# High-part products of a weight chunk first, low part waited for in mid chunk, in a split-precision decoder layer

## The chip, the core and the metric

The kernel runs on one core of one Trainium2 chip. The metric is the device time of one execution in microseconds, median of several runs. "Before" is the kernel without the change.

## What is computed

One inference step of one decoder layer, all in float32: 512 prompt tokens and 8 samples of one new token each, model width 1024.

```python
mod = silu(c) @ w_ada + b_ada                       # 9 vectors per sequence: shift, scale, gate x 3
x = x + 0.5 * ga1 * swiglu(rms_mod(x, g1, sh1, sc1), wf1i, wf1o)
h, state = mixer(rms_mod(x, g2, sh2, sc2), ...)     # RG-LRU branch and mLSTM branch, merged, projected
x = x + ga2 * h
x = x + 0.5 * ga3 * swiglu(rms_mod(x, g3, sh3, sc3), wf2i, wf2o)
y = rms(x, g_final)
```

`swiglu` is an up-projection to 2 x 2816 columns, silu of one half times the other, and a down-projection back to 1024. `w_ada` is 1024 x 9216.

## The kernel before, in words

**Layout.** Activations stand with features on the 128 partitions and all 520 tokens along the free side, in 8 row blocks of 128 features. Weights come from memory in chunks of 128 output columns: a chunk holds up to 8 blocks of 128 x 128, 512 KB.

**Split precision.** Every weight and activation is split into a high part in the fast matmul format and a low part, the rest. A product is high x high + high x low + low x high. SP loads a chunk into `raw` (line 418), ACT copies it into `w_h` (`split`, line 946, the copy on 955; in one place in two halves, 954 and 955), DVE subtracts it into `w_l` (`split`, line 1347, on 1354 and 1357). All three have a ring of 3 slots. ACT signals `w_hi_ready`, DVE `w_lo_ready`; both count chunks in order. SP loads the next chunk into a slot after DVE's signal, ACT overwrites `w_h` after TensorE's signal `chunk_done` of the chunk that used the slot before.

**Products.** `product` (line 585) multiplies one chunk with all 520 tokens, in two halves of 260 that lie in two PSUM banks of an accumulator tile `big`. For each row block it makes six matmuls: (w_h, x_h), (w_h, x_l), (w_l, x_h), each for two halves, 48 for 8 blocks. It waits for `w_lo_ready` ahead of everything (line 587), then for the accumulator to be emptied, and, where a list `ready` is given, ahead of each row block for the low part of the activations (line 594). Two accumulators alternate.

**Condition products.** `modulation` (line 610) makes one column block of `mod`: the silu of the conditions, 18 columns, is the stationary operand, a block of 128 weights moves, 16 matmuls a chunk, high and low part in turn (line 616), after a wait for `w_lo_ready` (line 613).

**Order of the work.** All engines run the same chunk list by hand-written loops. At the start, 17 of the 72 condition blocks are made from unsplit weights (line 691) while the first norm is computed; the first two chunks of the first up-projection have a function of their own (`first_products`, line 727). The first up-projection then runs 11 turns of 9 chunks in the order P M P M P M P M M (P a product, M a condition product; the first turn P P M M P M P M M). In a turn ACT splits chunk k+2 at step k; at step 7 it splits the next turn's first P in two halves. The first down-projection follows: 8 output tiles in three chunks of 8, 8 and 6 row blocks; the third chunk of every second tile has a `ready` list with one and the same value for its six blocks. Then the mixer, 81 chunks in straight-line code with the small matmuls of recurrence and attention between them (`small_job`; the recurrence gates are line 845), the second up-projection (44 P; the first P of each turn of 6 has a `ready` list), the second down-projection. The first two chunks after each norm of the residual are in `unnormalised` (line 632), with `ready`-like waits of its own. POOL, with the stored states and the first rows after a norm, waits in two places for `chunk_done`.

Of the kernel before, what the change touches and what calls it, by code (L numbers as in the profile page):

```python
# [20 lines left out]
P = 128  # L21
D = 1024
KT = D // P
# [3 lines left out]
HALF = T // 2  # L27
# [13 lines left out]
RING = 3  # L41
# [150 lines left out]
def build(nc, xT, cT, w_ada, b_ada, ff1_in, ff1_out, w_mix, ff2_in, ff2_out, vecs, conv_w, w_rg,  # L192
# [3 lines left out]
    with ctx:  # L196
        def sb(name, shape, dt=F32, stack=ctx):
            return stack.enter_context(nc.sbuf_tensor(name, shape, dt))

        def sem(name):  # L200
            return ctx.enter_context(nc.semaphore(name))
# [6 lines left out]
        w_h = [sb(f"w_h{i}", [P, KT * P], F32R) for i in range(RING)]  # L208
        w_l = [sb(f"w_l{i}", [P, KT * P], F32R) for i in range(RING)]
# [110 lines left out]
        w_hi_ready = sem("w_hi_ready")  # L320
        w_lo_ready = sem("w_lo_ready")
        chunk_done = sem("chunk_done")
# [261 lines left out]
        def _(pe):  # L584
            def product(c, c_expr, t, t_half, xh, xl, k0, n, first=True, last=True, ready=None):

                pe.wait_ge(w_lo_ready, c_expr + 1)
                if first and not (isinstance(t_half, int) and t_half == 0):
                    pe.wait_ge(evac[t % 2], t_half)
                out = big[t % 2]  # L590
                wh, wl = w_h[c % RING], w_l[c % RING]
                for i in range(n):
                    if ready is not None:
                        pe.wait_ge(lo_ready, ready(k0 + i))
                    w = slice(i * P, (i + 1) * P)
                    for s, (a, b) in enumerate(((wh, xh), (wh, xl), (wl, xh))):
                        for hf in range(2):
                            ins = nc.tensor.matmul(out[:, hf, 0:HALF], a[:, w],  # L598
                                                   b[:, k0 + i, hf * HALF:(hf + 1) * HALF],
                                                   start=first and i == 0 and s == 0,  # L600
                                                   stop=last and i == n - 1 and s == 2)
                ins.then_inc(chunk_done, 1)
# [7 lines left out]
            def modulation(c, c_expr, out, n):  # L610


                pe.wait_ge(w_lo_ready, c_expr + 1)
                for kt in range(KT):
                    for s, w in enumerate((w_h[c % RING], w_l[c % RING])):
                        ins = nc.tensor.matmul(out[0:NR, n * P:(n + 1) * P], cs_hl[:, kt, :],  # L616
                                               w[:, kt * P:(kt + 1) * P],
                                               start=kt == 0 and s == 0, stop=kt == KT - 1 and s == 1)
                ins.then_inc(chunk_done, 1)
# [123 lines left out]
            def ffn(cb, tbase, pattern, loops, s_xn, s_hid):  # L743
# [15 lines left out]
                def turn(i, pattern=pattern, k0=0):  # L759
                    n = a = 0  # L760
                    for k, kind in enumerate(pattern):
                        c = cb + k
                        if k < k0:
                            n += 1
                            continue
                        back = k == TURN_BACK and "M" in pattern and not (isinstance(i, int) and i == 0)
                        if back:
                            backs(i, "wait")
                        if kind == "P":
                            t = tbase + n  # L770
                            product(c, i * len(pattern) + c, t, i * (n_p // 2) + t // 2, xn_h, xn_l, 0, KT,
                                    ready=xn_split if k == 0 and not first else None)
                            n += 1
                        else:
                            g = sum(a >= t0 + size for t0, size in MOD_GROUPS)
                            m = M_ADA1 + g
                            if a == MOD_GROUPS[g][0]:
                                pe.wait_ge(taken[m % BANKS], i + m // BANKS)
                            modulation(c, i * len(pattern) + c, bank[m % BANKS], a - MOD_GROUPS[g][0])
                            a += 1  # L780
                        if back:
                            backs(i, "work")
# [16 lines left out]
                with pe.Fori(0, KT // 2) as i:  # L799
                    for jj in range(2):  # L800
                        for k, (k0, n) in enumerate(FFO_CHUNKS):
                            product(cb + 3 * jj + k, i * 6 + (cb + 3 * jj + k), tbase + jj,
                                    i + (tbase + jj) // 2, hid_h, hid_l, k0, n, first=k == 0, last=k == 2,
                                    ready=(lambda kt: s_hid + FT) if k == 2 and jj == 0 else None)
# [108 lines left out]
            for i, (what, j) in enumerate(MIX):  # L913
                if what == "bra":
                    xh, xl, base = hb_h, hb_l, S_HA
                elif what == "brb":
                    xh, xl, base = hb_h, hb_l, S_HB
                elif what == "out":
                    xh, xl, base = mg_h, mg_l, S_MG
                else:  # L920
                    xh, xl, base = xn_h, xn_l, S_XN2 + 1
                t = T_MIX + i
                if i == PRE:
                    product(C_MIX + i, C_MIX + i, t, t // 2, xh, xl, 0, KT, ready=lambda kt: S_XN2 + USABLE[kt])
                elif i > PRE:
                    product(C_MIX + i, C_MIX + i, t, t // 2, xh, xl, 0, KT, ready=(lambda kt: base + kt + 1)
                            if i == FIRST_OF[what] and what in ("bra", "brb", "out") else None)
                for key in AFTER[i]:
                    small_job(key)
# [1098 lines left out]
```

## Time and profile before

| | |
|---|---|
| median of 3 runs | 1464.92 us (1464.09 to 1465.06) |
| the profiled execution, its own time | 1464.09 us |
| its span, first to last instruction | 1462.3 us |
| TensorE matmul records | 1419.7 us, 11964 matmuls |
| DVE, ACT, POOL busy | 729.5, 558.8, 68.8 us |
| mean granted TensorE clock | 0.994 |

A matmul record reaches from its start to a modelled end, and records of successive matmuls overlap, so TensorE's busy time is not a measure of how well it is used; the distance between starts is. Idle time "before" an instruction is the gap to the end of the engine's last record, with the engine whose signal ended it.

### The profile page before, as it was taken

Reading aid. Unit: us, or ns where it says so; the run is one execution under the profiler, and the core shown is the slowest. Engines: PE = TensorE matmul, PEld = TensorE weight load, DVE = VectorE, ACT = ScalarE, POOL = GpSimd, SP = SyncE. Lnnn points to the kernel's source line nnn. Section 1 sums busy time; section 2 is a strip of 40 time slices with the busy share of each in tenths; the row PEclk is TensorE's granted clock in tenths of the full one; section 3 lists DMA queues with packets and bytes.
Section 4 is the critical chain, followed back from the end, with each engine's and each line's share of the span. In section 5 each row is a group of like instructions: output and inputs, shape, how many; then the busy total and the mean of one; then the engine's idle time right before and its main releaser. Section 6 shows DMA issues by size and latency. Waiting matters only on the chain.

```text
span 1462.3 us, 29304 instructions
## 1 busy us (share of the span) xinstructions
PE 1419.7 (97%) x11964; PEld 1384.7 (95%) x11964; DVE 729.5 (50%) x1250; ACT 558.8 (38%) x813; POOL 68.8 (5%) x135
## 2 busy tenths in 40 slices
PE   5999999999999989999999999999999999999996
PEld 4899999999999989999998989999999999999996
DVE  4645454455344665774475666744673333333333
ACT  4433444443232557723443435432452322221211
POOL 1000000000000300000011201200010000000000
PEclk9999999999999999999999999999999999999998
DMA  9455555555323422233253525432223223223321
GB/s 373 135 165 161 161 167 165 159 158 166 89 88 93 141 69 73 73 92 115 68 157 116 166 80 166 140 100 87 87 87 98 89 86 97 90 82 94 88 80 59
DMA packets 49588, 174.01 MB, mean 119 GB/s; under 512 B 6608, under 2 KB 6672, under 8 KB 49136
## 3 DMA queue, kind: packets, MB, share of 16 engines
q1 hardware_dynamic: 43200, 151.68, 33.5%
q0 software_dynamic: 6032, 19.25, 4.0%
q10 hardware_dynamic: 288, 2.13, 0.4%
q8 instruction: 49, 0.80, 0.2%
q14 instruction: 19, 0.16, 0.0%
HBM read 161.28 MB, written 11.75 MB: 118 GB/s over the span
## 4 chain that ended last, share of the span: by engine, by line
PE 90%; DVE 5%; ACT 2%; issue 1%; DMA 1%; POOL 0%; SPq 0%; DVEq 0%; ACTq 0%; POOLq 0%
PE big L598 79%; PE bank L616 2%; PE bank L885 2%; PE bank L877 1%; PE bank L891 1%; PE big L645 1%; DVE w_l L1357 1%; DMA adaw<-w_ada 1%; PE bank L845 1%; PE bank L909 1%; PE bank L864 0%; ACT w_h L954 0%; DVE tb L1918 0%; PE bank L691 0%; DVE tb L1561 0%
## 5 line engine op out<-in xcount | busy, mean ns | idle before, releaser
L1357 DVE TENSOR_TENSOR w_l<-raw,w_h 128x1024 fp32r<-128x1024 f32 (+2 forms) x272 | 321.5, 1186 | 355.4 <-ACT w_h L955 351.0
L598 PE MATMUL big<-xn_h,w_h 128*128 128x260 f32 x2224 | 452.9, 285 | 5.5 <-DVE w_l L1357 2.7
L598 PE MATMUL big<-xn_l,w_h 128*128 128x260 f32 x2224 | 449.7, 283 | 0.0
L598 PE MATMUL big<-xn_h,w_l 128*128 128x260 f32 x2224 | 448.1, 282 | 0.0
L955 ACT ACTIVATE w_h<-raw 128x1024 fp32r<-128x1024 f32 (+2 forms) x272 | 276.3, 1020 | 237.7 <-PE big L598 236.4
L598 PEld LDWEIGHTS big<-xn_h,w_h 128*128 128x128 f32 x2224 | 344.2, 188 | 9.6 <-issue 4.2
L598 PEld LDWEIGHTS big<-xn_h,w_l 128*128 128x128 f32 x2224 | 343.5, 188 | 0.0
L598 PEld LDWEIGHTS big<-xn_l,w_h 128*128 128x128 f32 x2224 | 343.3, 188 | 0.0
L598 PE MATMUL big<-hid_h,w_h 128*128 128x260 f32 x704 | 142.2, 283 | 0.0
L598 PE MATMUL big<-hid_h,w_l 128*128 128x260 f32 x704 | 141.5, 282 | 0.0
L598 PE MATMUL big<-hid_l,w_h 128*128 128x260 f32 x704 | 141.5, 282 | 0.0
L598 PEld LDWEIGHTS big<-hid_l,w_h 128*128 128x128 f32 x704 | 108.7, 188 | 0.0
L598 PEld LDWEIGHTS big<-hid_h,w_l 128*128 128x128 f32 x704 | 108.4, 188 | 0.0
L598 PEld LDWEIGHTS big<-hid_h,w_h 128*128 128x128 f32 x704 | 108.3, 188 | 0.0
L1476 DVE TENSOR_TENSOR tb<-tb,big 128x520 f32<-128x520 f32 x43 | 29.9, 696 | 124.3 <-PE big L598 124.3
L1052 ACT ACTIVATE tb<-big 128x520 f32<-128x520 f32 x43 | 26.0, 605 | 169.7 <-PE big L598 169.3
L616 PE MATMUL bank<-w_h,cs_hl 128*18 128x128 f32 x440 | 57.4, 223 | 0.5 <-DVE w_l L1357 0.5
L616 PE MATMUL bank<-w_l,cs_hl 128*18 128x128 f32 x440 | 57.3, 223 | 0.0
L968 ACT ACTIVATE tb<-x 128x520 f32<-128x520 f32 (+1 forms) x24 | 15.3, 639 | 104.7 <-DVE x L1458 82.0
L598 PE MATMUL big<-hb_h,w_h 128*128 128x260 f32 x256 | 51.7, 283 | 0.4 <-DVE ma L1877 0.4
L598 PE MATMUL big<-hb_h,w_l 128*128 128x260 f32 x256 | 51.5, 283 | 0.0
L598 PE MATMUL big<-hb_l,w_h 128*128 128x260 f32 x256 | 51.4, 282 | 0.0
(338 smaller groups left out, 1449.7 us busy)
## 6 DMA issues: line engine op xcount, KB each, us to landing
raw<-ff_in SPq DMA_DIRECT2D x88, 512.0 KB, 3.6
raw<-w_mix SPq DMA_DIRECT2D x81, 512.0 KB, 3.6
raw<-w_ada SPq DMA_DIRECT2D x55, 512.0 KB, 3.7
raw<-ff_out SPq DMA_DIRECT2D x32, 512.0 KB, 3.5
adaw<-w_ada SPq DMA_DIRECT2D x17, 512.0 KB, 14.2
cst_c<-st_C POOLq DMA_DIRECT2D x32, 256.0 KB, 4.4
o_Cs<-cst_c POOLq DMA_DIRECT2D x32, 256.0 KB, 3.4
raw<-ff_out SPq DMA_DIRECT2D x16, 384.0 KB, 3.2
```

The costliest lines, as they stand in the source:

```text
L598: ins = nc.tensor.matmul(out[:, hf, 0:HALF], a[:, w], b[:, k0 + i, hf * HALF:(hf + 1) * HALF], start=first and i == 0 and s == 0, stop=las ...
L616: ins = nc.tensor.matmul(out[0:NR, n * P:(n + 1) * P], cs_hl[:, kt, :], w[:, kt * P:(kt + 1) * P], start=kt == 0 and s == 0, stop=kt == KT ...
L645: ins = nc.tensor.matmul(big[t % 2][:, hf, 0:ZH], a[:, w], b[:, kt, hf * ZH:(hf + 1) * ZH], start=kt == 0 and s == 0, stop=kt == KT - 1 an ...
L845: ins = nc.tensor.matmul(out[:, 0:HALF], wrg[:, 0 if kind == "rga" else 1, a, :], rg_u[a % RG_BUFS][:, b * HALF:(b + 1) * HALF], start=Tru ...
L877: ins = nc.tensor.matmul(out[:, b * P:NP_], k_t[h % 2][:, dt, b * P:(b + 1) * P], q_t[h % 2][:, dt, b * P:NP_], start=dt == 0, stop=dt == ...
L885: ins = nc.tensor.matmul(out[:, c * P:NP_], lhs, dmat[:, c, c * P:NP_], start=c == 0, stop=c == CH - 1)
L891: ins = nc.tensor.matmul(out[:, 0:HD + 1], ktok[:, c, b * P:(b + 1) * P], vtok[:, c, :], start=c == 0, stop=c == CH - 1)
L955: A(w_h[c % RING][:, from_:width], raw[:, c % RING, from_:width], ACT.Copy).then_inc(w_hi_ready, 1)
L968: A(tb[2][:, :], x[:, kt, :], ACT.Square).then_inc(sq_ready, 1)
L1052: A(two(tb[0][:, :]), slot_view(t), ACT.Silu).then_inc(evac[t % 2], 1)
L1357: V.tensor_tensor(w_l[c % RING][:, from_:width], raw[:, c % RING, from_:width], w_h[c % RING][:, from_:width], ALU.subtract).then_inc(w_lo ...
L1476: V.tensor_tensor(two(tb[1][:, :]), two(tb[0][:, :]), slot_view(t), ALU.mult).then_inc(evac[t % 2], 1)
```

## The change

In `product`, where no `ready` list is given, the wait at the top is for the high part, all matmuls with `w_h` run first, then the wait for the low part, then all matmuls with `w_l`. With a `ready` list nothing changes. In `modulation` all eight matmuls with `w_h` run after a wait for the high part and the eight with `w_l` after a wait for the low part. `first_products` and `unnormalised` stay as they were. Number, shapes and operands of the matmuls stay the same.

```diff
             def product(c, c_expr, t, t_half, xh, xl, k0, n, first=True, last=True, ready=None):
 
-                pe.wait_ge(w_lo_ready, c_expr + 1)
+                pe.wait_ge(w_lo_ready if ready is not None else w_hi_ready, c_expr + 1)
                 if first and not (isinstance(t_half, int) and t_half == 0):
                     pe.wait_ge(evac[t % 2], t_half)
                 out = big[t % 2]
                 wh, wl = w_h[c % RING], w_l[c % RING]
+                if ready is None:
+                    for i in range(n):
+                        w = slice(i * P, (i + 1) * P)
+                        for b in (xh, xl):
+                            for hf in range(2):
+                                nc.tensor.matmul(out[:, hf, 0:HALF], wh[:, w],
+                                                 b[:, k0 + i, hf * HALF:(hf + 1) * HALF],
+                                                 start=first and i == 0 and b is xh, stop=False)
+                    pe.wait_ge(w_lo_ready, c_expr + 1)
+                    for i in range(n):
+                        w = slice(i * P, (i + 1) * P)
+                        for hf in range(2):
+                            ins = nc.tensor.matmul(out[:, hf, 0:HALF], wl[:, w],
+                                                   xh[:, k0 + i, hf * HALF:(hf + 1) * HALF],
+                                                   start=False, stop=last and i == n - 1)
+                    ins.then_inc(chunk_done, 1)
+                    return
                 for i in range(n):
                     if ready is not None:
                         pe.wait_ge(lo_ready, ready(k0 + i))
...
             def modulation(c, c_expr, out, n):
 
 
-                pe.wait_ge(w_lo_ready, c_expr + 1)
-                for kt in range(KT):
-                    for s, w in enumerate((w_h[c % RING], w_l[c % RING])):
+                for s, (ready, w) in enumerate(((w_hi_ready, w_h[c % RING]), (w_lo_ready, w_l[c % RING]))):
+                    pe.wait_ge(ready, c_expr + 1)
+                    for kt in range(KT):
                         ins = nc.tensor.matmul(out[0:NR, n * P:(n + 1) * P], cs_hl[:, kt, :],
                                                w[:, kt * P:(kt + 1) * P],
                                                start=kt == 0 and s == 0, stop=kt == KT - 1 and s == 1)
```

## Rows read from the trace of the kernel before

**Rows 1.** The page: busy time by engine, and the chain that ended last.
```profile
PE 1419.7 (97%) x11964; PEld 1384.7 (95%) x11964; DVE 729.5 (50%) x1250; ACT 558.8 (38%) x813; POOL 68.8 (5%) x135
...
PE 90%; DVE 5%; ACT 2%; issue 1%; DMA 1%; POOL 0%; SPq 0%; DVEq 0%; ACTq 0%; POOLq 0%
```
**Rows 2.** TensorE's waits: line, released by: us in total, times, longest us.
```profile
PE bank L845 <- ACT rg_r L1191: 5.8, 2, 4.4
PE big L598 <- DVE w_l L1357: 2.7, 11, 0.6
```
**Rows 3.** Timeline at a turn's border: start us, length us, engine, line; idle before in brackets.
```profile
95.39 0.61 ACT L955 ACTIVATE w_h<-raw 128x512 fp32r<-128x512 f32 x1
...
96.13 0.68 DVE L1357 TENSOR_TENSOR w_l<-raw,w_h 128x512 fp32r<-128x512 f32 x1
...
96.51 0.22 PE L616 MATMUL bank<-w_l,cs_hl 128*18 128x128 f32 x1
...
96.94 0.50 PE L598 MATMUL big<-xn_h,w_h 128*128 128x260 f32 x2 [0.21 <-DVE w_l L1357]
...
97.28 0.40 PE L598 MATMUL big<-xn_l,w_h 128*128 128x260 f32 x2
```
**Rows 4.** Timeline of TensorE in the turn before, at a border without a wait.
```profile
88.77 0.22 PE L616 MATMUL bank<-w_l,cs_hl 128*18 128x128 f32 x1
88.82 0.46 PE L598 MATMUL big<-xn_h,w_h 128*128 128x260 f32 x2
89.12 0.40 PE L598 MATMUL big<-xn_l,w_h 128*128 128x260 f32 x2
...
94.41 0.41 PE L598 MATMUL big<-xn_h,w_l 128*128 128x260 f32 x2
```
**Rows 5.** The chain that ended last, in order of time: first products of turns.
```profile
67.92 6.03 PE big L598 x48
...
96.94 6.04 PE big L598 x48
...
329.26 6.05 PE big L598 x48
```
**Rows 6.** Timeline at the start of the first up-projection.
```profile
48.80 2.05 ACT L955 ACTIVATE w_h<-raw 128x1024 fp32r<-128x1024 f32 x2
...
49.88 1.23 DVE L1357 TENSOR_TENSOR w_l<-raw,w_h 128x1024 fp32r<-128x1024 f32 x1 [0.97 <-ACT w_h L955]
...
50.43 0.23 PE L616 MATMUL bank<-w_l,cs_hl 128*18 128x128 f32 x1
...
51.16 0.24 PE L616 MATMUL bank<-w_h,cs_hl 128*18 128x128 f32 x1 [0.51 <-DVE w_l L1357]
...
52.91 0.39 PE L598 MATMUL big<-xn_h,w_h 128*128 128x260 f32 x1 [0.60 <-DVE w_l L1357]
```
**Rows 7.** Timeline, first down-projection: first pairs of third chunks and of the chunks after them.
```profile
371.37 0.40 PE L598 MATMUL big<-hid_h,w_h 128*128 128x260 f32 x2
...
375.70 0.40 PE L598 MATMUL big<-hid_h,w_h 128*128 128x260 f32 x2
...
387.23 0.40 PE L598 MATMUL big<-hid_h,w_h 128*128 128x260 f32 x2
...
391.56 0.40 PE L598 MATMUL big<-hid_h,w_h 128*128 128x260 f32 x2
```
**Rows 8.** Chain piece in the mixer; busy time of L598 in the second up-projection (PE, PEld, clock, DMA).
```profile
605.81 34.59 PE big L598 x288
...
1078.37:1318.87 240.50, 240.50 (x1993) 240.50 (x1993) 1.00 0.31 93
```
**Rows 9.** Recurrence gates by the timeline; a stretch by engine (PE, PEld, DVE, ACT, POOL, clock, DMA).
```profile
542.71 1.92 PE L845 MATMUL bank<-ma,wrg 128*128 128x260 f32 x8
...
549.02 3.49 PE L845 MATMUL bank<-ma,wrg 128*128 128x260 f32 x8 [4.40 <-ACT rg_r L1191]
...
549.40:552.80 3.40, 3.40 (x11) 2.79 (x10) 0.70 (x1) 2.25 (x6) 0.00 (x0) 0.50 0.43 143
```

## The prediction, made before the change was run

> **What bounds the kernel now.** The page first: TensorE is busy for 97% of the span and the chain that ended last runs over it for 90% [rows 1]. So the time is the sum of the matmuls plus the moments in which TensorE stands still, and a change that leaves every matmul in place can only win those moments back. I therefore read TensorE's list of waits next. Its largest waits on ACT lie at L845, in the recurrence gates of the mixer, which the change does not touch. On the low part of a weight chunk (w_l, made by DVE at L1357) the products at L598 wait 11 times, for 2.7 us in all [rows 2]; the condition products at L616 wait once more, 0.51 us [rows 6].
>
> That sum is too small, and the timeline says why. Matmul records overlap: pairs follow each other every 0.24 us while each pair's record lasts 0.40 us [rows 4]. An idle time is counted from the end of the record before, so about 0.16 us of each stop is invisible. I go by starts. At a border without a wait, the last condition matmul starts at 88.77, the product's first pair at 88.82 and its second at 89.12: 0.05 and 0.30 us [rows 4]. At a border with a wait the same steps take 96.51 to 96.94 and on to 97.28: 0.43 and 0.34 us [rows 3]. The stop costs 0.38 + 0.04 = 0.42 us, twice the 0.21 that the row shows as idle.
>
> Where these borders are: each turn of the first up-projection ends in two condition chunks in a row, which give ACT and DVE only 2 us for splitting the next product's weights. There are ten such borders (after each turn but the last), the first at 67.92, then nine from 96.94 to 329.26 at a distance of 29.04 us [rows 5]. The other two waits are at the start: the second condition chunk (51.16 after 50.43) and the product after it (52.91) [rows 6]. That makes the 11 and the one; no later product waits for w_l.
>
> **The change, part by part.**
>
> *First wait moved from low to high part.* At a border TensorE would be free at 96.51 + 0.06 = 96.57. The second half of the high part is written by ACT from 95.39 to 96.00 [rows 3], so 0.57 us before it is wanted; the low part is ready at 96.81. ACT and DVE are tied to the end of an earlier product, not to the start of this one, so this cover does not shrink when TensorE gets ahead. Each border then looks like 88.82, and I take 10 x 0.42 = 4.2 us.
>
> *Second wait, in mid chunk.* The low part is now asked for after 32 matmuls of 0.12 us, at 96.57 + 3.84 = 100.4, some 3.6 us after it is there. Behind that wait stand 16 matmuls and the chunk's completion signal, for which ACT and DVE (eviction, splitting into the slot that comes free) and one POOL wait are queued; with 3.6 us in hand none of them is delayed. If the cover went, the old wait would come back whole, 0.42 us a border. DMA issues are released by DVE's splits alone and move in no queue.
>
> *Condition chunks.* Eight matmuls with the high part (8 x 0.06 = 0.48 us) now come before the wait. It binds only at the second chunk: high part ready at about 49.83 (half of ACT's pair from 48.80), TensorE free at 50.49, high half to 50.97, then the low part, which DVE ends at 51.11. As before it starts at 51.16, but only eight matmuls are left: done at 51.64. The next product's high part was finished at 50.85, so it starts at 51.64 and not at 52.91: 1.27 us, and 0.04 for its first step as above, 1.31 together [rows 6].
>
> *A satisfied wait.* Every product without a readiness list and every condition chunk gets one more wait: 42 + 20 + 75 + 35 + 20 = 192 products and 55 condition chunks. What does one cost when it is satisfied? The down-projection answers: its third chunk of 36 matmuls has a wait before each of the six row blocks in one of two output tiles and none in the other. With six waits it takes 371.37 to 375.70, without 387.23 to 391.56, 4.33 us each [rows 7]. I take nothing. A rule of the Trainium skill can be held against this: TensorE: Matmul & The Clock Gate, Part 2, step 1, says that TensorE draws weight loads ahead of matmuls in flight, and a wait in mid stream is where that could stop. By the rows the sum stays at nothing; by the rule, read that way, every new wait would expose a load (priced as a rival below). [Rows 7] speak for the former.
>
> *The order itself.* Loads and matmuls are the same in kind and number: each matmul loads its weights anew before and after. What could shift is the step between matmuls. It is not constant: 34.59 us for 288 in the mixer, 0.1201, but 240.50 for 1993 in the second up-projection, 0.1207 [rows 8]; 89.12 to 94.41 for 44 is 0.1202 [rows 4]. Same shapes, same order, two values; nothing in the trace says which the new order gets. I take no change, being between the ends. If all went to 0.1207, the reordered 7440 matmuls outside the second up-projection would cost 7440 x 0.0006 = 4.4 us; if all went to 0.1200, 1680 x 0.0007 + 2016 x 0.0002 = 1.6 us would be won.
>
> *The clock.* After TensorE's 4.40 us stop at 549 us the granted clock is 0.50 (1.2 GHz) for 3.4 us, and eight matmuls take 3.49 us that took 1.92 just before [rows 9]. All of this arrives 5 us earlier afterwards, and the fall may be missed or be met at another stop: about 2 us either way (1.57 on these eight, the rest on the product behind them). I count nothing.
>
> **Sum:** 4.2 + 1.31 = 5.5 us less. The profiled execution took 1464.09 (span 1462.3 and 1.8 around it), hence 1458.6. The median of the three runs is 0.83 above it, so I forecast **1459.4**. Its own range is 1459.4 - 1.6 - 2 to 1459.4 + 2.
>
> **The rivals.**
>
> 1. *The step turns slow.* The new order falls into the slower of the two steps everywhere: 1459.4 + 4.4 = 1463.8, within 0.2% of before. For it: the first products after a stop in the second up-projection start a slow stretch that never ends. Against: most stretches run at the fast one. Chance 0.10.
>
> 2. *The wait moves to the high part.* If ACT were more than 0.57 us later at the borders, the product would wait for w_h as long as for w_l now; only the 1.31 us of the start would stay: 1463.6. Against: its order of work does not change. Chance 0.03.
>
> 3. *The other side: each mid-chunk wait exposes a weight load, even when satisfied.* Place: the seam between high and low part of all 192 products. Price: after a stop the first step is 97.28 - 96.94 = 0.34 for a pair and not 0.24 [rows 3, 4], so 0.10 us a seam, 19.2 us; condition chunks at 0.04 add 2.2. That would give 1459.4 + 21.4 = 1480.8. It decides from (5.5 + 2.9) / 247 = 0.034 us a wait. Against it stand the six waits that cost nothing [rows 7]; for it, that those were on a signal long given, while this one is given 3.6 us before. Chance 0.05.
>
> 4. *It does not do what it says*: the borders wait for something else behind w_l, such as the eviction of the accumulator. By the code that tile is emptied before the product ahead of the border ends, so chance 0.02; 1464.9.
>
> **How the numbers follow.** 0.80 is left for the forecast. 0.2% of 1464.9 is 2.9 us, about what a measurement can tell from no change: under 1462.0 counts as faster. The forecast's own range, 1455.8 to 1461.4, lies under that, rivals 1, 2 and 4 within 0.2% of before, rival 3 above: faster 0.80, same 0.15, slower 0.05. The range runs from the low end, 1455.8, to 1463.9, which takes in rivals 1 and 2 and leaves out 3 and 4.
>
> **What the profile after would show.** Right: no wait of L598 or L616 on w_l but for one short one at 51 us; product starts 28.6 us apart from turn to turn and not 29.04; the first product at 51.6; chunks elsewhere as long as before. Wrong: a step over 0.24 us between the last pair with the high part and the first with the low part in every chunk (rival 3); the same chunk lengths at 0.1207 a matmul in the mixer (rival 1); a wait on w_h at the turn borders (rival 2). The forecast falls if the turns keep 29.0 us, or if the time after 360 us grows.

## The result, and the profile after

| | before | after |
|---|---|---|
| time, median (lowest to highest), us | 1464.99 (1464.09 to 1467.37, 4 runs) | 1454.4 (1453.1 to 1456.43, 4 runs) |
| profiled execution / its span, us | 1464.09 / 1462.3 | 1453.86 / 1452.1 |

The ratio is 0.9926, with a 95% interval of 0.9909 to 0.9944. The change is faster by 10.6 us: the direction is as forecast, the gain about twice the forecast 5.5, and the time 1.4 us under the low end of the range.

In the changed kernel the reordered products are L597 (high part) and L604 (low part), products with a readiness list L615, condition products L633, the split L972 (ACT) and L1374 (DVE), the recurrence gates L862. First the page, busy times and the chain that ended last:

```profile
PE 1412.8 (97%) x11964; PEld 1379.8 (95%) x11964; DVE 729.4 (50%) x1250; ACT 559.2 (39%) x813; POOL 68.6 (5%) x135
...
PE 92%; DVE 4%; ACT 2%; issue 1%; DMA 1%; POOL 0%; SPq 0%; ACTq 0%; DVEq 0%; POOLq 0%
```

Beside [rows 1], the number of matmuls and loads is the same, yet TensorE's busy time fell by 6.9 us. Waits account for little of that. Of the forecast's 5.5 us, 2.7 + 0.5 stood as idle time before [rows 2, 6], and only the other 2.3, hidden under the overlap of records, can leave the busy time. This row alone says that something else than the waits moved. The waits of TensorE after (line, released by, us in total, times, longest):

```profile
PE bank L862 <- ACT rg_r L1208: 5.8, 2, 4.4
...
PE big L754 <- DVE w_l L1374: 0.4, 1, 0.4
PE big L597 <- DVE ma L1894: 0.4, 1, 0.4
```

The 11 waits of [rows 2] on w_l are gone; the only one on w_l left in the list is that of the very first products (L754), whose code the change doesn't touch. A border of the first up-projection on the timeline, the one that [rows 3] show before:

```profile
92.31 0.61 ACT L972 ACTIVATE w_h<-raw 128x512 fp32r<-128x512 f32 x1
...
93.05 0.68 DVE L1374 TENSOR_TENSOR w_l<-raw,w_h 128x512 fp32r<-128x512 f32 x1
...
93.48 0.45 PE L597 MATMUL big<-xn_h,w_h 128*128 128x260 f32 x2
93.77 0.40 PE L597 MATMUL big<-xn_l,w_h 128*128 128x260 f32 x2
...
97.36 2.09 PE L604 MATMUL big<-xn_h,w_l 128*128 128x260 f32 x16
```

The product starts at 93.48, 0.25 us before DVE has ended the low part (93.05 + 0.68 = 93.73), with no idle time in brackets; the low part is wanted at 97.36, 3.6 us after it is there. Its first step is 0.29 us as at the borders of [rows 4]. From 93.48 eight more turns lead to 321.51, so they are 228.03 / 8 = 28.50 us apart, where 28.6 was forecast and 29.04 stood before [rows 5]. Now the start, which [rows 6] show before:

```profile
29.66 0.51 PE L754 MATMUL big<-xn_h,w_h 128*128 128x260 f32 x2 [0.44 <-DVE w_l L1374]
...
49.34 0.64 PE L633 MATMUL bank<-w_h,cs_hl 128*18 128x128 f32 x8
50.02 0.65 PE L633 MATMUL bank<-w_l,cs_hl 128*18 128x128 f32 x8
50.51 0.45 PE L597 MATMUL big<-xn_h,w_h 128*128 128x260 f32 x2
```

The product that began at 52.91 begins at 50.51, 2.40 us earlier. The short wait that was forecast at 51 us is there, hidden under the overlap of records: the last line of L633 starts 0.68 us behind the one ahead of it, where eight matmuls take 0.48. Not all of the 2.40 us is the change's: the very first products already begin at 29.66 and not at 30.80, ahead of anything that was changed. The chain of before, then that of after (start, length), and the windows around the four matmuls of L704 (before) and L721 (after); in a window the third number from the end is the granted clock:

```profile
2.83 11.93 DMA adaw<-w_ada
...
27.52 1.06 PE bank L704 x4
```
```profile
2.92 11.27 DMA adaw<-w_ada
...
26.85 0.60 PE bank L721 x4
```
```profile
27.20:28.50 1.30, 1.30 (x13) 0.72 (x5) 0.00 (x0) 0.98 (x2) 0.00 (x0) 0.50 1.01 403
```
```profile
26.85:27.45 0.60, 0.60 (x8) 0.43 (x12) 0.00 (x0) 0.60 (x1) 0.00 (x0) 1.00 1.01 403
```

Half of the 1.14 us is a transfer that ended at 14.19 and not at 14.76. The other half is the clock: before, it fell to 0.50 here, and four small matmuls took 1.06 us that took 0.60 after, at 1.00; the rest of the half lies on those just ahead of them. The change gave 2.40 - 1.14 = 1.26 us here, where 1.27 was forecast (1.31 with the product's first step).

So the waits gave what was expected of them: ten borders 4.24 us by their starts (one 0.435, nine 0.371, and 0.047 on each first step), with the start 5.5. The other half is in the steps between matmuls. A window from the first matmul of one chunk to the first of a later one, divided by the matmuls between, gives the mean step. The rows (window; length; busy time and count of PE, PEld, DVE, ACT, POOL; granted clock, DMA share, GB/s) are 20 chunks of the mixer (960 steps), 41 chunks of the second up-projection (1968) and seven output tiles of the second down-projection (924). Before:

```profile
938.65:1053.92 115.27, 115.27 (x963) 115.27 (x961) 63.49 (x107) 37.84 (x55) 3.19 (x6) 1.00 0.33 100
1081.34:1318.87 237.53, 237.53 (x1971) 237.53 (x1969) 79.04 (x85) 67.36 (x91) 0.00 (x0) 1.00 0.31 94
1324.64:1435.71 111.07, 111.07 (x926) 111.07 (x925) 36.44 (x56) 25.95 (x30) 0.00 (x0) 1.00 0.28 82
```

After, the same chunks:

```profile
930.19:1045.18 114.99, 114.99 (x962) 114.99 (x961) 63.53 (x107) 37.84 (x55) 3.18 (x6) 1.00 0.34 101
1072.59:1308.23 235.64, 235.64 (x1970) 235.64 (x1969) 79.06 (x85) 67.31 (x91) 0.00 (x0) 1.00 0.31 95
1313.97:1424.56 110.59, 110.59 (x926) 110.59 (x925) 36.43 (x56) 25.95 (x30) 0.00 (x0) 1.00 0.28 82
```

There is no wait in any of these windows, before or after: TensorE is busy for the whole of each, at full granted clock, with the same work on the other engines. Still the second up-projection goes from 237.53 / 1968 = 120.70 to 119.74 ns a step, the down-projection from 120.21 to 119.69, the mixer from 120.07 to 119.78. Over the whole kernel, chunk by chunk, that is 5.4 us: second up-projection 1.9, mixer 1.2, first up-projection 1.2, the two down-projections 0.55 each.

The balance of the two profiled executions: 1.1 (landing and clock at the start) + 1.3 (waits at the start) + 4.2 (borders) + 5.4 (steps) = 12.0 us less, and 1.9 more, of the clock at two later places (below): 10.1, against 10.2 between the spans.

### The profile page after: what moved, and what is told of

Read it like the earlier page. It is cut to its first block, busy times and chain, and to the rows that moved or that the text cites. A ratio compares the mean times of both kernels' runs of the same rounds, so it can differ in the third digit from the quotient of the medians.

```text
span 1452.1 us, 29304 instructions
## 1 busy us (share of the span) xinstructions
PE 1412.8 (97%) x11964; PEld 1379.8 (95%) x11964; DVE 729.4 (50%) x1250; ACT 559.2 (39%) x813; POOL 68.6 (5%) x135
## 4 chain that ended last, share of the span: by engine, by line
PE 92%; DVE 4%; ACT 2%; issue 1%; DMA 1%; POOL 0%; SPq 0%; ACTq 0%; DVEq 0%; POOLq 0%
PE big L597 49%; PE big L604 24%; PE big L615 6%; PE bank L633 4%; PE bank L902 2%; PE bank L894 1%; PE bank L908 1%; PE big L662 1%; DMA adaw<-w_ada 1%; PE bank L862 1%; PE bank L926 1%; PE bank L881 0%; DVE tb L1935 0%; PE bank L708 0%; PE big L754 0%
## 5 line engine op out<-in xcount | busy, mean ns | idle before, releaser
L1374 DVE TENSOR_TENSOR w_l<-raw,w_h 128x1024 fp32r<-128x1024 f32 (+2 forms) x272 | 321.6, 1187 | 347.9 <-ACT w_h L972 343.6
L597 PE MATMUL big<-xn_h,w_h 128*128 128x260 f32 x2096 | 424.4, 284 | 0.0
L597 PE MATMUL big<-xn_l,w_h 128*128 128x260 f32 x2096 | 422.6, 283 | 0.0
L972 ACT ACTIVATE w_h<-raw 128x1024 fp32r<-128x1024 f32 (+2 forms) x272 | 276.3, 1020 | 236.7 <-PE big L604 231.5
L597 PEld LDWEIGHTS big<-xn_h,w_h 128*128 128x128 f32 x2096 | 324.0, 189 | 1.5
L597 PEld LDWEIGHTS big<-xn_l,w_h 128*128 128x128 f32 x2096 | 323.0, 189 | 0.0
L604 PE MATMUL big<-xn_h,w_l 128*128 128x260 f32 x2096 | 273.2, 283 | 0.0
L604 PEld LDWEIGHTS big<-xn_h,w_l 128*128 128x128 f32 x2096 | 261.2, 188 | 0.0
L597 PE MATMUL big<-hid_h,w_h 128*128 128x260 f32 x608 | 122.1, 282 | 0.0
L597 PE MATMUL big<-hid_l,w_h 128*128 128x260 f32 x608 | 121.9, 282 | 0.0
L597 PEld LDWEIGHTS big<-hid_h,w_h 128*128 128x128 f32 x608 | 93.4, 188 | 0.0
L597 PEld LDWEIGHTS big<-hid_l,w_h 128*128 128x128 f32 x608 | 93.4, 188 | 0.0
L604 PE MATMUL big<-hid_h,w_l 128*128 128x260 f32 x608 | 79.2, 282 | 0.0
L604 PEld LDWEIGHTS big<-hid_h,w_l 128*128 128x128 f32 x608 | 75.7, 188 | 0.0
L597 PE MATMUL big<-hb_h,w_h 128*128 128x260 f32 x224 | 45.2, 283 | 0.4 <-DVE ma L1894 0.4
L597 PE MATMUL big<-hb_l,w_h 128*128 128x260 f32 x224 | 45.1, 282 | 0.0
L1077 ACT ACTIVATE hid_h<-tb 128x520 f32 (+1 forms) x43 | 27.3, 635 | 37.1 <-DVE tb L1493 37.1
L633 PE MATMUL bank<-w_l,cs_hl 128*18 128x128 f32 x440 | 35.3, 222 | 0.0
```

What stands on the lines that cost most here:

```text
L597: nc.tensor.matmul(out[:, hf, 0:HALF], wh[:, w], b[:, k0 + i, hf * HALF:(hf + 1) * HALF], start=first and i == 0 and b is xh, stop=False)
L604: ins = nc.tensor.matmul(out[:, hf, 0:HALF], wl[:, w], xh[:, k0 + i, hf * HALF:(hf + 1) * HALF], start=False, stop=last and i == n - 1)
L972: A(w_h[c % RING][:, from_:width], raw[:, c % RING, from_:width], ACT.Copy).then_inc(w_hi_ready, 1)
L1077: A(hid_h[:, i * (n_p // 2) + (t - tbase) // 2, :], tb[1][:, :], ACT.Copy).then_inc(hi_ready, 1)
L1374: V.tensor_tensor(w_l[c % RING][:, from_:width], raw[:, c % RING, from_:width], w_h[c % RING][:, from_:width], ALU.subtract).then_inc(w_lo ...
```

## The experiments

Theory 1 was: the waits gave what was forecast, and the other half is the order of the matmuls, which shortens the step by itself; theory 2 is its rival. Theories 3 to 7 came up as the runs went on; each expectation says what its theory gives. Steps are mean distances between the starts of matmuls within chunks, in ns.

**Order alone.** The change with all waits back where they were (the edit is against the changed kernel, as are all below that don't say otherwise; where a loop is rewritten, only the new lines that matter are shown):

```diff
-                pe.wait_ge(w_lo_ready if ready is not None else w_hi_ready, c_expr + 1)
+                pe.wait_ge(w_lo_ready, c_expr + 1)
...
-                    pe.wait_ge(w_lo_ready, c_expr + 1)
...
-                for s, (ready, w) in enumerate(((w_hi_ready, w_h[c % RING]), (w_lo_ready, w_l[c % RING]))):
-                    pe.wait_ge(ready, c_expr + 1)
+                pe.wait_ge(w_lo_ready, c_expr + 1)
+                for s, w in enumerate((w_h[c % RING], w_l[c % RING])):
```

> The order of the change with the waits of before: product and condition chunk wait for the low part at the top, then all high-part matmuls, then all low-part ones. Theory 1 (two gains that add: the waits some 5.5 us, and a shorter step between matmuls that comes from the order alone): about 1460 us, 0.997 of before; the twelve waits on w_l are back, the step is 119.6 ns in the second up-projection and 119.5 in the second down-projection. Theory 2 (the step is shorter because of the late wait, which lets the engine run ahead): as before, 1465 us, step 120.7 and 120.2 ns.

1459.58 us (1459.02 to 1461.2, 6 runs), ratio 0.9969 (0.9957 to 0.9981): 4.9 us less than the 1464.49 of before beside it. Its waits on w_l, and its window over the second up-projection:

```profile
PE big L597 <- DVE w_l L1373: 2.9, 11, 0.6
```
```profile
1079.22:1314.86 235.64, 235.64 (x1971) 235.64 (x1969) 79.03 (x85) 67.33 (x91) 0.00 (x0) 1.00 0.31 95
```

The eleven waits stand as in [rows 2], and the window is that of the change to the hundredth.

**Waits alone.** Matmuls in the old order, waits as in the change (the low part is asked for ahead of the first matmul that uses it):

```diff
+                    steps = [(l, b, i, hf) for i in range(n) for l, b in ((0, xh), (0, xl), (1, xh)) for hf in range(2)]
...
+                        if is_l and not waited:
+                            pe.wait_ge(w_lo_ready, c_expr + 1)
...
-                for s, (ready, w) in enumerate(((w_hi_ready, w_h[c % RING]), (w_lo_ready, w_l[c % RING]))):
-                    pe.wait_ge(ready, c_expr + 1)
-                    for kt in range(KT):
+                pe.wait_ge(w_hi_ready, c_expr + 1)
+                for kt in range(KT):
+                    for s, (ready, w) in enumerate(((w_hi_ready, w_h[c % RING]), (w_lo_ready, w_l[c % RING]))):
+                        if kt == 0 and s == 1:
+                            pe.wait_ge(w_lo_ready, c_expr + 1)
```

> The order of before, row block by row block, with the waits of the change: high part at the top, low part ahead of the first matmul that uses it (after 4 matmuls of a product, after 1 of a condition chunk). At a turn's border the low part is ready at 96.81 and would be asked for at 96.57 + 0.48, so the border waits go; the condition chunk at 51 us keeps its wait. Theory 1: 4.2 at the borders and 1.31 - 0.48 at the start, 5.0 us less than before, about 1460 us, step as before (120.7 ns in the second up-projection, 120.2 in the down-projection). Theory 2: 1454.5 us, step 119.6 and 119.5 ns.

1459.52 us (1458.57 to 1460.01, 6 runs), ratio 0.9965 (0.9953 to 0.9977): 5.0 us less. In its second up-projection:

```profile
1077.08:1314.60 237.52, 237.52 (x1970) 237.52 (x1969) 79.04 (x85) 67.36 (x91) 0.00 (x0) 1.00 0.31 94
```

The window is that of before. So 4.9 + 5.0 = 9.9 us make up the 10.6 of the change within their intervals, and neither half needs the other: theory 1 holds, theory 2 falls. Four matmuls of cover (0.48 us) give at the borders all that 32 give: in both kernels the product starts there 0.06 us behind the last condition matmul. At the start they give less: counted from the very first products, the next product begins 0.45 us later than with the change and then stops 0.4 us for its own low part.

**Two other orders.** Why does the order matter? If a seam between two weight parts cost time, an order with more seams would be slower. "Product major" runs the whole high part with xn_h, then with xn_l, then the low part; "tight seams" changes the weight part within every half row block, 32 seams a chunk:

```diff
+                    steps = [(l, b, i, hf) for l, b in ((0, xh), (0, xl), (1, xh)) for i in range(n) for hf in range(2)]
```
```diff
+                    steps = [(l, b, i, hf) for i in range(n) for hf in range(2) for l, b in ((0, xh), (1, xh), (0, xl))]
```

> As the change, but the high part runs as two passes: (w_h, x_h) for all row blocks, then (w_h, x_l) for all, then (w_l, x_h). One seam between w_h and w_l a chunk as in the change (15 before), 23 changes of weight block instead of 15. Theory 3 (the step follows the number of seams between the two weight tiles): step at 119.6 ns or under. Theory 4 (it follows how often the weight block changes): longer than in the change, by half of what a change costs. Theory 5 (it follows the sequence of addresses, no count): anything from 119 to 121, not the same in the up- and the down-projection.

> Each row block and half by itself: (w_h, x_h), (w_l, x_h), (w_h, x_l): 32 seams a chunk and more, low part waited for after one matmul. Theory 3: before to the change is 14 seams and 26 to 53 ns a chunk, 2 to 4 ns a seam, so some 17 more seams give 30 to 65 ns a chunk over before: step 120.9 to 122 ns. Theory 5: no such order. In either the waits at the turn borders are gone.

One run of each: 1450.4 and 1454.64 us. Their second up-projections, product major first:

```profile
1070.75:1306.16 235.41, 235.41 (x1970) 235.41 (x1969) 79.02 (x85) 67.40 (x91) 0.00 (x0) 1.00 0.31 95
```
```profile
1074.03:1308.96 234.93, 234.93 (x1970) 234.93 (x1969) 79.03 (x85) 67.31 (x91) 0.00 (x0) 1.00 0.31 95
```

The order with most seams has the shortest window of the three (119.38 ns a step), so a seam is not what costs: theory 3 falls. Theory 4 is not borne out, since product major is no slower than the change. Part of the expectation for tight seams was a miss: its border waits were not gone. At the border of the same turn its timeline shows

```profile
94.87 0.33 PE L600 MATMUL big<-xn_h,w_h 128*128 128x260 f32 x1
95.17 0.39 PE L600 MATMUL big<-xn_h,w_l 128*128 128x260 f32 x1
95.39 0.28 PE L600 MATMUL big<-xn_l,w_h 128*128 128x260 f32 x1
```

The low part is asked for after two steps' time instead of 32 and is late by little: the first two steps take 0.30 + 0.22 us and not the 0.17 + 0.12 of the change, 0.23 us a border.

**Addresses instead of order.** All orders give steps from 119 to 121 ns, and for one kernel they repeat to 0.02 ns from run to run. What an order changes, and a wait does not, is which weight block and which moving block follow each other, and so at which addresses. If that is the cause, the old order must change its step when only addresses move. Two unused strips in the kernel of before shift w_l by 32 bytes (and the tiles laid out behind it by 64), or by 64 (and 128); no instruction is changed (this edit is against the kernel of before):

```diff
+        sb("pad_a", [P, 8])
         w_l = [sb(f"w_l{i}", [P, KT * P], F32R) for i in range(RING)]
+        sb("pad_b", [P, 8])
```

(with 16 in place of 8 in the second).

> The kernel before, but the three w_l tiles lie 32 bytes further on in every partition (what follows them 64 bytes); no instruction changes. Theory 5 (the step follows from how the addresses of successive loads and moving operands fall): the step in the second up-projection leaves 120.72 ns by more than 0.3, and so does that in the mixer or the down-projection. Theory 6 (it follows from the order of the operands as such, which tile comes after which): unchanged, 120.7, 120.15 and 120.2 ns. The time moves by 48 x 40 x the change of the step in each stage; waits as before.

> The same with 64 bytes. Theory 5: a change too, unless addresses count only within 64 bytes, in which case the steps are those of before to 0.05 ns. Theory 6: unchanged.

One run of each: 1457.61 and 1463.62 us. Second up-projections, 32 bytes first:

```profile
1077.65:1313.26 235.61, 235.61 (x1970) 235.61 (x1969) 79.03 (x85) 67.31 (x91) 0.00 (x0) 1.00 0.32 95
```
```profile
1082.11:1318.54 236.43, 236.43 (x1970) 236.43 (x1969) 79.05 (x85) 67.32 (x91) 0.00 (x0) 1.00 0.31 95
```

The kernel of before, in its own order and with all of its waits, runs this stretch at 119.72 ns where it took 120.70, and at 120.14 with the other shift. Thirty-two bytes give what the order gave here: theory 6 falls, and theory 5 stands in that the step follows the addresses, though not them alone (last section). Of the four tiles that TensorE reads in this stretch, xn_h, xn_l, w_h and w_l, only w_l lies behind a strip; the tiles of the other engines that moved with it were not held still.

**Timed again, and order and shift together.** The change and product major in five rounds; the change, product major and the kernel with late waits alone (the old order), each with the 32-byte strips:

```diff
+        sb("pad_a", [P, 8])
         w_l = [sb(f"w_l{i}", [P, KT * P], F32R) for i in range(RING)]
+        sb("pad_b", [P, 8])
```

> The product-major order again, timed. Its steps were 119.3 to 119.6 ns against 119.5 to 119.8 for the change; 0.3 ns on the 2016 matmuls of the first up-projection and 0.2 on the mixer's 3600 are 1.3 us: about 1 us under the change, 1453 us.

> The change itself, timed beside the product-major order: 1454.4 us, steps 119.6 and 119.5 ns as in its first profile.

> The change, with w_l 32 bytes further on as in the shift of the kernel before. Theory 5 (the step is set by how addresses fall, so order and shift do not add): steps anywhere from 119.2 to 120.2 ns, not 0.9 under those of the change; time between 1450 and 1457 us. Theory 7 (order and shift each take away a loss of their own, and add): steps near 118.8 ns, about 1446 us.

> Product-major with the same 32 bytes. Theory 5: steps from 119.2 to 120.2 ns, 1449 to 1456 us. Theory 7: near 118.7 ns, about 1445 us.

> The order of before with late waits, and 32 bytes: no matmul changes its place. If waits and addresses are all there is to the gain, both are had here: 1459.5 less what the shift gave the kernel before (about 7 us, one run), so 1452.5 to 1453.5 us, as fast as the change; steps 119.8 in the second up-projection and 119.5 in the first, as in the shifted kernel before. If the order had something of its own: over 1456 us.

| kernel | time, us (lowest to highest) | ratio (95%) | step, second up-projection | step, second down-projection |
|---|---|---|---|---|
| product major | 1452.52 (1452.05 to 1453.03) | 0.9919 (0.9905 to 0.9933) | 119.62 | 119.76 |
| the change | 1453.36 (1453.07 to 1455.59) | 0.9928 (0.9914 to 0.9942) | 119.73 | 119.68 |
| the change, 32 bytes on | 1455.0 (1454.06 to 1455.84) | 0.993 (0.9917 to 0.9944) | 119.80 | 120.17 |
| product major, 32 bytes on | 1454.1 (1452.67 to 1455.22) | 0.9923 (0.991 to 0.9937) | 120.08 | 119.71 |
| late waits, old order, 32 bytes on | 1452.61 (1451.86 to 1455.66) | 0.9919 (0.9906 to 0.9933) | 119.71 | 119.95 |

The shift that shortens the steps of the old order lengthens some of those of the new orders: the two do not add, and theory 7 falls. With the tiles 32 bytes on, the change's order even has the longer steps of the two: 119.80 against 119.71 and 120.17 against 119.95 ns. The last line is the most telling: old order, late waits, 32 bytes:

```profile
1071.37:1306.97 235.60, 235.60 (x1970) 235.60 (x1969) 79.04 (x85) 67.32 (x91) 0.00 (x0) 1.00 0.31 95
```

Without any reordering in the products it is as fast as the change. Neither it nor product major beats the change by more than the executions of one kernel differ; they are 0.8 us under it, with intervals that overlap.

**One block for all.** The last run holds the addresses still within a chunk (from chunk to chunk the slot of w_h and the accumulator still change). In the reordered products every matmul loads the first block of the high part and moves the first half row block, so the kernel leaves these products out of the computation:

```diff
-                                nc.tensor.matmul(out[:, hf, 0:HALF], wh[:, w],
-                                                 b[:, k0 + i, hf * HALF:(hf + 1) * HALF],
+                                nc.tensor.matmul(out[:, hf, 0:HALF], wh[:, 0:P],
+                                                 xh[:, k0, 0:HALF],
...
-                            ins = nc.tensor.matmul(out[:, hf, 0:HALF], wl[:, w],
-                                                   xh[:, k0 + i, hf * HALF:(hf + 1) * HALF],
+                            ins = nc.tensor.matmul(out[:, hf, 0:HALF], wh[:, 0:P],
+                                                   xh[:, k0, 0:HALF],
```

> The change, but every reordered product loads one and the same weight block and moves one and the same half row block, 48 times a chunk (so the products are not those of the reference; the number and shape of the matmuls are). Theory 5: with no address changing, the step is one value, repeated without the swing of 114 to 131 ns, the same in both up-projections, and it need not be the mean of the others. Theory 8 (the swing comes from elsewhere, say the other engines' traffic): the swing stays.

One run: 1448.82 us. The second up-projection and seven turns of the second down-projection:

```profile
1069.99:1304.00 234.01, 234.01 (x1971) 234.01 (x1970) 79.03 (x85) 67.38 (x91) 0.00 (x0) 1.00 0.31 95
1309.75:1420.71 110.96, 110.96 (x926) 110.96 (x925) 36.42 (x56) 25.98 (x30) 0.00 (x0) 1.00 0.28 82
```

With constant addresses the single steps, read from the starts in the trace, are regular: 120 ns on the hidden tile of the down-projections, in all but a few behind each unchanged product, and a pattern of 117 to 121 that repeats every fifteen steps (mean 118.67) on the tile of the up-projections. In the change they run from 115 to 131 in the second up-projection, without a short period. So half of the expectation came true (the irregularity comes from the addresses, and theory 8 falls, since the other engines went on as before) and half was a miss (a swing of four ns stays with one of the tiles). Matmuls of one shape on two tiles, each with its addresses held fixed, have two steps: that again is in the line of theory 5.

## Why the prediction was half right

**First wait moved.** Right: 4.2 us forecast, 4.24 measured. Counting by starts and not by the idle time in brackets was what made this right; the idle times of [rows 2] would have given half.

**Condition chunks.** Right: 1.27 us forecast for the start of the product, 1.26 measured. It was forecast at 51.6 and came at 50.51, 1.14 us of which lies ahead of the change, at the start.

**Second wait, and a satisfied wait.** Right at nothing. At a seam of the down-projection after, high part to low part:

```profile
361.24 0.40 PE L597 MATMUL big<-hid_l,w_h 128*128 128x260 f32 x2
361.48 0.64 PE L604 MATMUL big<-hid_h,w_l 128*128 128x260 f32 x4
```

0.24 us for the pair with the wait behind it, as for any other pair, and the change without its mid-chunk waits (order alone) has the same window over the second up-projection, 235.64 us: rival 3 did not occur. The Trainium skill (TensorE: Matmul & The Clock Gate, Part 2, step 1) says that weight loads can be drawn ahead of matmuls in flight. That a satisfied wait in mid stream would stop this, the reading held against the change, this trace does not show. Rival 2 did not occur (no wait on w_h in the list), nor rival 4.

**The order itself: the step that failed.** It was put at nothing, with bounds of +4.4 and -1.6 us, and it gave -5.4. What was wrong was not the doubt but the bounds. The two values of [rows 8], 0.1200 and 0.1207, were taken for the two steps that there are, and the new order was to get one or the other. The runs show that the step moves with the addresses and not only with the order: over the orders and layouts tried it lies from 119.4 to 120.7 ns in the second up-projection, and the new order's 119.7 is below both values that before had to show. The sign could not have been read from the trace of before, and rival 1 (all steps slow) was as open as what came; that the new order got the shorter steps is the luck of this layout, since 32 bytes on it has the longer ones. But the size could have been bounded better: two steps of one shape that differ by 0.6% in a stretch without waits say that something that the row doesn't name sets them, and 7440 + 1680 reordered matmuls times 0.7 ns are 6.4 us either way. The low end, 1459.4 - 6.4 - 2 = 1451.0, would then have held the result.

**The clock.** The term of about 2 us either way came out on the losing side, 1.9 us at two places; the start, where the clock gave back half of the 1.14 us, was not thought of. Windows after (columns as above):

```profile
539.10:545.90 6.80, 5.44 (x17) 4.67 (x18) 0.98 (x2) 5.38 (x11) 0.00 (x0) 0.50 0.25 80
1436.80:1442.00 5.20, 3.91 (x17) 3.86 (x18) 0.75 (x2) 0.27 (x1) 0.00 (x0) 0.50 0.00 0
```

and before, at the end:

```profile
1450.50:1452.50 2.00, 1.93 (x10) 1.96 (x10) 0.00 (x0) 0.00 (x0) 0.00 (x0) 0.51 0.00 0
```

After the same stop of the recurrence gates the granted clock is 0.50 (1.2 GHz) for 6.8 us, where it was for 3.4 [rows 9]. At the end it is 0.50 for the last 5.2 us of TensorE's work, where it was for the last 2. The sums of the last norm, after:

```profile
1437.41 2.29 PE L685 MATMUL bank<-ones,ssq 128*128 128x1 f32 x10 [2.65 <-DVE ssq L1388]
```

and before:

```profile
1448.62 1.28 PE L668 MATMUL bank<-ones,ssq 128*128 128x1 f32 x10 [2.65 <-DVE ssq L1371]
```

Both come after a stop of 2.65 us, and only those of after find the clock at half. About 1 us lies at each place. The executions of the changed kernel differ by 3.3 us; the shortest, 1453.1, has a mean granted clock of 0.994 and the longest, 1456.43, one of 0.991. Why the same stops are followed by longer or shorter stretches at half clock was not followed up.

## What to carry to other kernels

Count a removed wait by the distances between starts, and it will come out as forecast: here 5.5 us of 5.5. Where an engine is busy without a break, a new order of the same instructions is not free in either direction: bound it by how far the step of equal instructions varies anywhere in the trace, and take the ends beyond the values seen. And before a gain is put down to an order, move the tiles by a few bytes in the old order: if that gives the same, the order has nothing of its own, and a cheap strip of padding is a thing to try by itself (here 32 bytes gave it, 64 bytes half of it in the second up-projection).

## What the runs showed of the hardware that was not expected

Equal matmuls (128x128 weights, 260 columns) at full granted clock, with no wait between, follow each other at steps that depend on where the blocks lie: 120.70 ns became 119.72 when one set of tiles moved by 32 bytes, and 120.14 when it moved by 64, with all that lies behind them moved by twice as much. The products of L615, whose order the change leaves alone, shortened in the second up-projection (120.72 to 120.15 ns) and lengthened in the second down-projection (120.29 to 120.54), with nothing changed but what runs ahead of them.

The distance from chunk to chunk repeats over a long stretch: for 48 matmuls it is 5793 ns in the second up-projection before and 5740 in most of it after. One order at one set of addresses can hold two such distances. Before, products on xn_h and xn_l run at 5793 behind the norms and at 5760 behind the recurrence gates; here are 96 matmuls of each:

```profile
506.51:518.10 11.59, 11.59 (x98) 11.59 (x97) 9.70 (x17) 6.48 (x11) 2.07 (x4) 1.00 0.44 136
558.31:569.83 11.52, 11.52 (x99) 11.52 (x97) 8.99 (x16) 6.36 (x10) 1.21 (x4) 1.00 0.16 46
```

With late waits alone, where order and addresses are those of before, and the other engines work as much, the first of these stretches takes 11.53 us, one 5772 and one 5760:

```profile
502.40:513.93 11.53, 11.53 (x98) 11.53 (x97) 9.69 (x17) 6.47 (x11) 2.06 (x4) 1.00 0.44 135
```

That is the pair of values in [rows 8] that the prediction could not explain, and it means that the addresses alone do not fix the step: by these runs and by L615, what ran ahead seems to count too. How the addresses set the step inside the chip, and what chooses between the two values, was not tried and stays open.
